# Attention on one Trainium2 core: value products in bursts of four key tiles, with five buffers of turned probabilities

## The reference, cut to what matters

```
p_cmp = masked_softmax(q @ k_cmp + bias, dc >= 0);      o_cmp = p_cmp @ v_cmp      # 64 slots
p_slc = masked_softmax(q @ k_slc + bias, selected);     o_slc = p_slc @ v_slc      # 4 blocks of 64 keys
p_win = masked_softmax(q @ k_win + bias, 0<=dist<256);  o_win = p_win @ v_win
out = g0 * o_cmp + g1 * o_slc + g2 * o_win;  return out @ w_o
```

## Time and profile before

| | us |
|---|---|
| time, median of 3 runs (lowest, highest) | 4170.05 (4166.51, 4170.34) |
| the profiled execution, its own time | 4168.69 |
| its span in the trace | 4166.7 |
| the attention stage in it | 1369 to 1877 |
| TensorE busy over the span | 3978.3 (95%) |
| VectorE, ScalarE, GpSimd busy | 2361.2, 1627.1, 424.2 |

### The profile page before, as it was taken

How to read it: one execution, slowest core, us unless ns; L and a number is a source line. 1 busy time by engine, 2 the same in 40 slices (tenths; PEclk the granted TensorE clock), 3 DMA queues, 4 the chain that set the end, 5 groups by cost and what they waited for, 6 DMA issues and landing times.

```text
span 4166.7 us, 63444 instructions
## 1 busy us (share of the span) xinstructions
PE 3978.3 (95%) x23002; PEld 3471.3 (83%) x23002; DVE 2361.2 (57%) x3482; ACT 1627.1 (39%) x2260; POOL 424.2 (10%) x439
## 2 busy tenths in 40 slices
PE   8999999998998789899699999999999999999998
PEld 7888888886787556667599999999999999999987
DVE  4444444445443677753455555555566666666678
ACT  3222222222342577782223333233334444444455
POOL 2000000000231244440100010010010100001010
PEclk9999999999999799999799999999999999999999
DMA  5223232223544211005433343353355555556577
GB/s 220 101 91 111 92 137 94 91 91 147 171 152 143 84 47 42 26 19 183 163 131 121 137 145 141 121 172 133 147 185 190 199 190 186 202 185 212 184 257 264
DMA packets 153671, 594.27 MB, mean 143 GB/s; under 512 B 26896, under 2 KB 54928, under 8 KB 113043
## 3 DMA queue, kind: packets, MB, share of 16 engines
q1 hardware_dynamic: 139076, 548.02, 36.2%
q0 software_dynamic: 10384, 35.14, 3.0%
q10 hardware_dynamic: 4080, 9.44, 0.6%
HBM read 535.76 MB, written 57.83 MB: 142 GB/s over the span
## 4 chain that ended last, share of the span: by engine, by line
PE 49%; DVE 1%; DMA 0%; issue 0%; ACT 0%; POOL 0%; DVEq 0%; POOLq 0%; SPq 0%; ACTq 0%
PE moe_ps L443 10%; PE moe_ps L445 10%; PE moe_ps L444 10%; PE moe_ps L485 5%; PE moe_ps L486 5%; PE moe_ps L487 5%; PE moe_ps L424 1%; PE moe_ps L452 0%; PE moe_ps L453 0%; PE moe_ps L456 0%; DMA moe_wd_raw<-in_moe_wd 0%; DVE moe_yacc L364 0%; DMA moe_stage<-h_moe,moe_ids 0%; DVE moe_ht_lo L323 0%; DVE moe_gu_lo L327 0%
## 5 line engine op out<-in xcount | busy, mean ns | idle before, releaser
L443 PE MATMUL moe_ps<-moe_ht_hi,moe_gu_hi 128*128 128x256 f32 (+4 forms) x3136 | 936.6, 299 | 1.6 <-DVE moe_ht_lo L323 1.6
L445 PE MATMUL moe_ps<-moe_ht_hi,moe_gu_lo 128*128 128x256 f32 (+4 forms) x3136 | 936.1, 298 | 0.0
L444 PE MATMUL moe_ps<-moe_ht_lo,moe_gu_hi 128*128 128x256 f32 (+4 forms) x3136 | 935.6, 298 | 0.0
L244 ACT CAST moe_gu_hi<-moe_gu_raw 128x2048 fp32r<-128x2048 f32 x226 | 431.0, 1907 | 521.5 <-PE moe_ps L445 490.4
L327 DVE TENSOR_TENSOR moe_gu_lo<-moe_gu_raw,moe_gu_hi 128x2048 fp32r<-128x2048 f32 x226 | 517.2, 2289 | 170.4 <-ACT moe_gu_hi L244 169.0
L443 PEld LDWEIGHTS moe_ps<-moe_ht_hi,moe_gu_hi 128*128 128x128 f32 x3136 | 596.2, 190 | 5.4 <-issue 1.8
L444 PEld LDWEIGHTS moe_ps<-moe_ht_lo,moe_gu_hi 128*128 128x128 f32 x3136 | 597.0, 190 | 3.5
L445 PEld LDWEIGHTS moe_ps<-moe_ht_hi,moe_gu_lo 128*128 128x128 f32 x3136 | 596.0, 190 | 0.0
L364 DVE SCALAR_TENSOR_TENSOR moe_yacc<-moe_ps,job_weights,moe_yacc 128x512 f32<-128x512 f32 x504 | 374.7, 749 | 327.1 <-PE moe_ps L487 327.1
L485 PE MATMUL moe_ps<-moe_wd_hi,moe_hid_hi 128*128 128x512 f32 x1008 | 395.9, 393 | 0.0
L486 PE MATMUL moe_ps<-moe_wd_lo,moe_hid_hi 128*128 128x512 f32 x1008 | 393.3, 390 | 0.0
(11 more groups left out here) (355 smaller groups left out, 6600.6 us busy)
## 6 DMA issues: line engine op xcount, KB each, us to landing
moe_gu_raw<-in_moe_wgu SPq DMA_DIRECT2D x228, 1024.0 KB, 4.8
moe_wd_raw<-in_moe_wd SPq DMA_DIRECT2D x112, 1024.0 KB, 6.7
first_gu<-in_ffn_wgu SPq DMA_DIRECT2D x58, 1024.0 KB, 4.8
ffn_wd_raw<-in_ffn_wd SPq DMA_DIRECT2D x28, 1024.0 KB, 6.8
kvq_lo<-qt SPq DMA_DIRECT2D x8, 1024.0 KB, 5.0
kt<-kt_rows SPq DMA_DIRECT2D x8, 1024.0 KB, 6.2
shared<-in_w_kvq SPq DMA_DIRECT2D x5, 1024.0 KB, 8.1
kvq_raw<-in_w_kvq SPq DMA_DIRECT2D x5, 1024.0 KB
```

The lines of the kernel that those rows point to most:

```text
L244: act.copy(gu_hi[s][:, :, :, :].rearrange("p a k c -> p (a k c)"), gu_raw[r][:, :]).then_inc(s_gu_hi, 1)
L443: pe.matmul(out[:, 0:W], gu_hi[s][:, half, k, :], ht_hi[:, k, 0:W], start=(k == 0), stop=False)
L444: pe.matmul(out[:, 0:W], gu_hi[s][:, half, k, :], ht_lo[:, k, 0:W], start=False, stop=False)
L445: last = pe.matmul(out[:, 0:W], gu_lo[s][:, half, k, :], ht_hi[:, k, 0:W], start=False, stop=(k == KT - 1))
```

## The change

Value products stand in bursts of four tiles in place of two. The burst is issued behind the turn of tile m = 5, 9, 13, ..., and has tiles m - 5 to m - 2. The buffers of turned probabilities become five, and the copy of tile m waits for the product of tile m - 5. `copy_out(u)` moves on ScalarE to the place behind the copy of the tile behind whose turn the burst with the unit's last product stands.

```diff
-        pt = [sb(f"pt{s}", [P, R, P]) for s in range(4)]
+        BURST, PT = 4, 5
+        pt = [sb(f"pt{s}", [P, R, P]) for s in range(PT)]
...
+        put_at, begun_at = [], 0
+        for m in range(first_pt[-1]):
+            if m - 1 - begun_at >= BURST:
+                put_at += [m] * (m - 1 - begun_at)
+                begun_at = m - 1
+        put_at += [first_pt[-1]] * (first_pt[-1] - begun_at)
...
-                if m >= 4:
-
-                    act.wait_ge(s_pv, m - 3)
+                if m >= PT:
+
+                    act.wait_ge(s_pv, m - PT + 1)
...
-                    if m == first_pt[u] + min(3, len(key_tiles(u)) - 1) and u >= 1:
-                        copy_out(u - 1)
+                    for done in range(4 * TILES):
+                        if m == put_at[first_pt[done + 1] - 1] + 1:
+                            copy_out(done)
                     copy_pt(m)
...
                     transpose_p(m)
-                    if m >= 3 and m % 2:
-                        values(m - 3)
-                        values(m - 2)
+                    for done in range(first_pt[-1]):
+                        if put_at[done] == m:
+                            values(done)
```

More of the change, by code:

```diff
@@ L1638, in _ @@
                 values_part(4 * TILES - 1, b)
-            copy_out(4 * TILES - 1)
+            for done in range(4 * TILES):
+                if put_at[first_pt[done + 1] - 1] + 1 >= first_pt[-1]:
+                    copy_out(done)
         @block.vector
@@ L1852, in values @@
                     last = pe.matmul(o_ps[u % 2][parity * DH:(parity + 1) * DH, 0:2 * P].rearrange("p (a q) -> p a q", a=2), v,
-                                     pt[m % 4][0:rows, parity:R:2, :], start=start, stop=stop)
+                                     pt[m % PT][0:rows, parity:R:2, :], start=start, stop=stop)
                 last.then_inc(s_pv, 1)
@@ L1877, in _ @@
                 values_part(4 * TILES - 1, b)
-            for m in range((first_pt[-1] - 2) // 2 * 2, first_pt[-1]):
-                values(m)
+            for done in range(first_pt[-1]):
+                if put_at[done] == first_pt[-1]:
+                    values(done)
 def project_out(nc, ot_rows, w_o, x1, gain, router, ident, x2_rows, h_rows, logits, shared, s_wo_first, s_ot_out):
```

2 lines of the change are left out of this document (1 added, 1 removed).

## The result

| | before | after | predicted |
|---|---|---|---|
| time, median (lowest to highest), 6 runs each on one chip | 4169.97 (4165.76 to 4172.78) | 4185.15 (4181.93 to 4187.67) | 4166.5 (4157 to 4173) |
| span of the profiled execution | 4166.7 | 4183.9 | |

The ratio is 1.004, with a 95% interval of [1.003, 1.005]. The change made the kernel slower by 0.4%, where no change to speak of was forecast; the time lies outside the range. The stage itself is 22.6 us longer in the trace than it was.

What follows compares the result with a forecast made beforehand. TensorE, busy 95% of the span, was taken as the bound. Terms of -6.6 (free part), +1.4 and +1.7 gave -3.5 us: 4165.2 from the profiled 4168.69, 4166.5 from the median 4170.05; range 4157 to 4173.

Steps and rivals of the forecast that it cites:

- The price of a burst: On TensorE, each burst saved takes away 0.32 us (0.26 to 0.38); 64 fewer save 20.5 us of work.
- The head swallows what is taken from it: At unit heads, 13.9 us less TensorE work only lengthens waits for VectorE and ScalarE, from some 44 to about 58.
- fixed parts: From a unit's last turned tile to the last step where TensorE had waited; product work there costs nothing.
- in the free part it costs its full time: Behind the last waiting step, up to the last turned tile, product work counts fully: 5.2 - 11.8 = -6.6 us.
- Term (2): Attention stage: steps that come earlier meet a release they just missed before; +1.7 us, bounds 0 and 13.8.
- Term (1): Stage's tail: with two PSUM tiles, the third of four turned tiles waits for the first's copy; +1.4 us (+0.45 to +1.8).
- Term (3): On ScalarE, a copy waits for its burst's first product, holding queued exponentials; taken as 0, without cover 32 us.
- rival C: ScalarE's held copies reach TensorE, 0.5 us per uncovered hold; with 20 of them 4176.5; chance 0.08.
- Term (4): `copy_out` behind the burst on ScalarE, and SP's later loads and stores, cost 0.
- Unit 30, +0.55: Last block: the head loses two free products, the back gains two and loses a burst, lengthening the unit by 0.55 us.
- Rival A: Heads are not fixed, so the whole burst saving arrives: 4151, or 4159.6 with half of the swallowed part; chance 0.16.
- Rival B: Longer head waits lower the clock, 1.7 us per new spell; with seven spells 4178.4; chance 0.06.

Runs made afterwards that it cites:

- h1_head: Kernel before, five buffers, block 2's query load before unit 1's store, products behind each unit's last turned tiles moved into the next burst; 4180.99, ratio 1.0026.
- e2_six: Changed kernel with six buffers of turned probabilities in place of five, small VectorE tiles sharing space; 4192.13, ratio 1.0051, 4 runs only.
- h2_back: Kernel before, five buffers, query load moved, bursts merged into fours except the pair behind each unit's last turned tiles; 4175.62, ratio 1.0013.
- i1_four_all: e1_query with ScalarE's copies ahead of the exponential and the scaling in every step; 4173.37, ratio 1.0011 to the kernel before.
- the sizes 1 to 4: Changed kernel's code with bursts of one, two, three or four tiles, query load moved except with two: 4195.40, 4170.00, 4176.43, 4178.74.
- e1_query: Changed kernel with the load of block 2's queries issued ahead of the store of unit 1 on SP; 4178.74, ratio 1.0022 to the kernel before.
- f2_two_cf: Changed kernel's code with bursts of two, and ScalarE's copies ahead of the exponential in even steps; 4165.01, ratio 0.9986 to the kernel before.
- f1_four_cf: e1_query with ScalarE's copies moved ahead of the exponential in even steps; 4181.95, ratio 1.0029 to the kernel before.

## Why the prediction was wrong

- **The price of a burst: right.** 0.32 was forecast. By the undisturbed steps of both traces TensorE's list got 21.4 us shorter for 64 bursts, 0.33 each. A burst of four in the back of unit 30 takes 1.88 from start to start, four products of 0.43 and 0.16 for the edge behind them; the prediction had 0.15 there:

```profile
1860.87 1.95 PE L1863 MATMUL att_o<-att_pt,first_sum 128*64 128x256 f32 x16
1862.75 1.20 PE L1821 MATMUL att_s<-kt,kvq_lo 128*128 128x512 f32 x4
```

 The Trainium skill, "TensorEngine Tiling (Array Packing)", Key Properties, says that a change of the tiling mode drains TensorE. The loader's idle 0.17 ahead of and 0.38 behind a burst of 128x64 products agree; no run here shows the drain itself.

- **The head swallows what is taken from it: right.** +12.9 against 13.9 by the table, whose heads end at step 3; in the prediction's own fixed parts of units 9 to 31, 15.5 more waits for 12.7 less work. In unit 30 VectorE and ScalarE keep their times to 0.01 us, and h1_head shows it alone.

- **"In the back of a unit TensorE runs without a pause", so "in the free part it costs its full time": this is the step that failed.** It was read from a trace in which the products stood there. I took a stretch without waits for one without limits, and counted a net gain of 6.6 us (4.4 to 8.9) from 37 edges fewer in it. Measured, the free parts of units 9 to 31 have 5.5 us less work and 13.4 us more waits. But a turn may not start before ScalarE has copied the tile two before, and that copy stands behind an exponential or a scaling. In unit 25 of the changed kernel the chain from the end of score step 4 through VectorE, the exponential and the copy to the end of the turn two tiles later takes 3.74 us by the semaphores (1753.23 to 1756.96). Before, with the pair (turn 1737.30, products, next turn 1738.99):

```profile
1737.30 0.60 PE L1836 MATMUL att_t<-ident,att_p_win 128*128 128x128 f32 x4
1737.83 0.65 PE L1852 MATMUL att_o<-att_pt,vc 64*64 64x256 f32 x4
1738.40 0.65 PE L1852 MATMUL att_o<-att_pt,att_vw 128*64 128x256 f32 x4
1738.99 0.66 PE L1836 MATMUL att_t<-ident,att_p_slc 128*128 128x128 f32 x4
1739.48 1.06 PE L1795 MATMUL att_s<-kct,kvq_lo 128*128 128x128 f32 x8
1740.47 0.66 PE L1836 MATMUL att_t<-ident,att_p_slc 128*128 128x128 f32 x4
```

 and in the changed kernel without it:

```profile
1753.40 0.60 PE L1847 MATMUL att_t<-ident,att_p_win 128*128 128x128 f32 x4
1753.84 0.60 PE L1847 MATMUL att_t<-ident,att_p_slc 128*128 128x128 f32 x4
1754.66 1.16 PE L1806 MATMUL att_s<-kct,kvq_lo 128*128 128x128 f32 x8 [0.22 <-DVE att_neg_max L1766]
1756.30 0.66 PE L1847 MATMUL att_t<-ident,att_p_slc 128*128 128x128 f32 x4 [0.48 <-ACT att_pt L1599]
...
1763.46 0.66 PE L1847 MATMUL att_t<-ident,att_p_slc 128*128 128x128 f32 x4 [0.48 <-ACT att_pt L1599]
```

 From the first turn shown to the third it is 3.17 with two products in between and 2.90 with none. The list is 1.25 shorter there (1.69 from the first turn to the second, now 0.44) and 0.27 are gained; then the products stand behind and cost their full time again. The last row is the same at the next pair of steps, where nothing had waited before: 2.89 from the turn at 1760.57 to it, against 2.93 with the two products in between (1743.75 to 1746.68 before).

- **Term (2), "steps that come earlier meet a release", +1.7 with a bound of 13.8: mis-sized.** This is the term in which the failed step should have been paid for. With the other score steps the waits of units 9 to 31 outside the heads grew by 16.9, of which 2.2 in the tail: 14.7. That is over the bound, since I had bounded the wait by the edges saved and not by the products that move away with them. A product that is taken from a place where it covered a wait saves nothing there, and costs its 0.43 in full where it goes.

- **Term (1), the tail: right** in kind, 2.2 against 1.4, but over its bound of 1.8. The matmuls' idle times there are 0.86, 0.33 and 0.24, the last two inside the bounds for one; the first is longer, because ScalarE was behind when the tail began:

```profile
1884.20 0.60 PE L1844 MATMUL att_t<-ident,att_p_cmp 128*64 128x128 f32 x4 [0.86 <-ACT att_pt L1599]
...
1888.55 1.06 PE L1847 MATMUL att_t<-ident,att_p_slc 128*128 128x128 f32 x8 [0.33 <-ACT att_pt L1599]
...
1892.91 1.14 PE L1847 MATMUL att_t<-ident,att_p_slc 128*128 128x128 f32 x8 [0.24 <-ACT att_pt L1599]
```

- **Term (3), the hold of a copy, and rival C: 0 was right** to within the 0.7 us of e2_six. The sign named for C, a turn that waits for ScalarE in the back of units, did show, but with ScalarE's own work as the cause and not the hold.

- **Term (4), the copy-out and SP "have a block of queries in hand: 0": wrong by 6.9 us.** True of every block but block 2, whose load stands behind the store of unit 1 in the first units. I had looked at SP in the middle of the stage only.

- **Unit 30, +0.55: measured +0.84** (18.66 to 19.50 from last turned tile to last turned tile). The list gave 0.55; 0.11 is a turn's wait for a copy, 0.15 a second edge inside the bursts (below) that had lain under a wait, 0.02 the ring.

- **Rival A** (the whole saving arrives) is excluded by the heads. **Rival B** (the clock) is at most 6.8 of the trace's 22.6 us, not shown to come from the change, and nothing in the medians.

In sum the stage came out 26.1 us above the forecast of -3.5: 10.5 at the turned tiles (13.6 less the 3.1 that the terms 1 and 2 had), 3.3 at other steps, 14.5 in the first units, less 1.0 at the heads and 0.9 of work (rounded apart). Settled by runs are the cover (h2_back, i1_four_all, the sizes 1 to 4), the heads (h1_head) and the queries (e1_query). Open are what is left in the first units and the 5.4 us outside the stage. Of the first, 7.2 us in e1_query, up to 6.8 can be the clock (13.7 us more at 1.2 GHz there), and f2_two_cf, with pairs and the same long spell, has 5.0; in f1_four_cf it is 4.9 with 3.4 more at 1.2 GHz. A third PSUM tile for the turns, which would attack the cover's cause itself, was not tried.

## What to carry to other kernels

A stretch in which the bounding engine never pauses may be free of waits because of the very instructions that one wants to move: before counting a move there as free, take the chain through the other engines (here turn, exponential, copy, turn, 3.7 us) and see what is left of the cover without them. Merging small groups saves their edges and makes gaps between the groups; the best size is where one more edge costs as much as the gap, here two tiles, with three perhaps level. And read every queue behind a moved step at its first use too, where nothing is in hand yet.

## What the runs showed of the hardware

- A burst of products with 64 columns of weights (128x64) between turns with 128x128 costs 0.33 us for both edges together.
- Within a burst the compressed tile (64x64 weights) beside a 128x64 one costs 0.15 at the change: 0.58 from start to start in place of 0.43. The loader's idle time of 0.39 stands behind it:

```profile
1855.46 0.19 PEld L1863 LDWEIGHTS att_o<-att_pt,vc 64*64 64x64 f32 x4 [0.17 <-issue]
1856.04 1.06 PEld L1863 LDWEIGHTS att_o<-att_pt,att_vw 128*64 128x64 f32 x12 [0.39 <-issue]
```

- From 1394 on in the stage, spells at 1.2 GHz lasted 3.4, 6.8, 10.2, 20.5 and once 23.9 us in all these kernels, 37.5 to 61.4 us together. Which of them a kernel has does not follow the size of its bursts. One spell of 10.2 more is worth up to 5.1 us, as much as the smaller effects of this study.
